# Convolution products placed around the head copies, and one reciprocal moved behind a maximum, in the attention phase of an encoder layer

## The reference, cut to what matters

```python
a = u[..., :C_CONV] * jax.nn.sigmoid(u[..., C_CONV:])
a = conv(a, conv_w, width 31, depthwise) + conv_b          # 1024 tokens x 512 channels
...
s = einsum('bqhd,bkhd->bhqk', q, k) * scale                # 8 heads, 96 wide, 1024 x 1024
p = softmax(s);  o = einsum('bhqk,bkhd->bqhd', p, v)       # v is 64 wide
```

## Time and profile before

| | |
|---|---|
| runs of the kernel | 1921.9 us median of 3 (1918.92 to 1922.35) |
| the profiled execution | 1919.46 us, its span 1917.3 us |
| PE busy | 1840.7 us (96%) |
| DVE busy | 1389.1 us (72%) |
| ACT busy | 796.2 us (42%) |
| POOL busy | 802.1 us (42%) |
| mean granted TensorE clock | 0.986 of full |

### The profile page before, as it was taken

The page is one execution under the profiler, slowest core; times in us unless marked ns, Lnnn a source line. Parts: engine busy times, 40 slices in busy tenths (PEclk is TensorE's granted clock), DMA queues, the critical chain, the costliest instruction groups (busy, mean ns, idle before and its releaser), DMA issues.

```text
span 1917.3 us, 22679 instructions
## 1 busy us (share of the span) xinstructions
PE 1840.7 (96%) x8043; PEld 1471.1 (77%) x8043; DVE 1389.1 (72%) x1774; ACT 796.2 (42%) x1248; POOL 802.1 (42%) x605
## 2 busy tenths in 40 slices
PE   4999999999999999997999998999999999999997
PEld 3788888888888878985665656877888888888886
DVE  6778888885777686776888886358656555577778
ACT  4532232223344554246776643154332323334443
POOL 1076655665200010029999941014566556520000
PEclk8999999999999999997999999999999999999999
DMA  9046666545753442000000023112233323476333
GB/s 351 19 138 199 209 220 198 192 160 206 255 194 97 131 160 71 1 1 0 1 1 0 3 73 144 66 55 91 102 110 110 110 83 110 170 251 226 99 106 126
DMA packets 132795, 232.11 MB, mean 121 GB/s; under 512 B 8780, under 2 KB 66227, under 8 KB 132434
## 3 DMA queue, kind: packets, MB, share of 16 engines
q1 hardware_dynamic: 132500, 230.73, 35.5%
q10 hardware_dynamic: 190, 0.01, 0.0%
HBM read 177.75 MB, written 52.95 MB: 120 GB/s over the span
## 4 chain that ended last, share of the span: by engine, by line
PE 35%; POOL 7%; issue 6%; DVE 5%; DMA 1%; ACT 1%; POOLq 0%; ACTq 0%; DVEq 0%
PE ps L502 19%; PE ps L854 9%; PE ps L2753 4%; POOL cv L1816 3%; PE ps L376 1%; POOL cv L1815 1%; PE ps L1657 1%; POOL slot L1766 1%; PE ps L1635 1%; DVE T L935 1%; POOL rqk L1751 0%; DMA wor<-in_w_out 0%; DVE wo L1926 0%; DVE grow L1673 0%; DVE ring L479 0%
## 5 line engine op out<-in xcount | busy, mean ns | idle before, releaser
L502 PE MATMUL ps<-T,ring 128*128 128x512 f32 x1920 | 441.8, 389 | 0.0
L502 PEld LDWEIGHTS ps<-T,ring 128*128 128x128 f32 x1920 | 360.3, 188 | 75.1 <-DVE ring L479 0.2
L502 PE MATMUL ps<-B,ring 128*128 128x512 f32 x1440 | 339.6, 392 | 4.1 <-DVE SG L561 3.8
L502 PEld LDWEIGHTS ps<-B,ring 128*128 128x128 f32 x1440 | 270.5, 189 | 63.9 <-issue 8.0
L954 POOL TENSOR_SCALAR stat<-stat 128x1 f32<-128x1 f32 x32 | 10.5, 329 | 548.7 <-ACT XS L879 257.8
L568 POOL TENSOR_TENSOR HID<-HID,SG 128x512 f32<-128x512 f32 x80 | 122.1, 1527 | 262.3 <-DVE HID L553 151.5
L854 PE MATMUL ps<-PW 128*128 128x512 f32 x924 | 217.3, 389 | 0.0
L854 PE MATMUL ps<-PT 128*128 128x512 f32 x900 | 212.0, 390 | 0.0
L854 PEld LDWEIGHTS ps<-PW 128*128 128x128 f32 x924 | 173.3, 188 | 36.0
L479 DVE TENSOR_TENSOR ring<-sums,ring 128x512 fp32r<-128x512 f32 x160 | 162.4, 1024 | 52.6 <-ACT ring L473 52.6
L854 PEld LDWEIGHTS ps<-PT 128*128 128x128 f32 x900 | 168.5, 188 | 34.8
(11 more groups left out here) (337 smaller groups left out, 3313.1 us busy)
## 6 DMA issues: line engine op xcount, KB each, us to landing
adat<-ffn_hidden SPq DMA_DIRECT2D x154, 256.0 KB, 2.7
ada_raw<-in_w_ada SPq DMA_DIRECT2D x56, 512.0 KB, 4.0
rawg<-in_ffn_wg SPq DMA_DIRECT2D x22, 1024.0 KB, 5.5
rawu<-in_ffn_wu SPq DMA_DIRECT2D x22, 1024.0 KB, 5.3
ffn_hidden<-HID SPq DMA_DIRECT2D x84, 256.0 KB, 2.8
ffn_hidden<-base SPq DMA_DIRECT2D x66, 256.0 KB, 2.6
H<-in_x SPq DMA_DIRECT2D x16, 512.0 KB, 6.6
h_saved_rows<-H SPq DMA_DIRECT2D x16, 512.0 KB, 2.6
```

The lines of the kernel that those rows point to most:

```text
L502: mm = e.matmul(ps[:, product_bank(M, k)], ring[:, place % RING, wx, kc], RIGHT[k][:, xx, kc], start=(kc == 0 and i == 0), stop=(kc == HC ...
```

## The change

Products are dealt out anew, seven to an even unit and three to an odd one, where it was six and four. A second table, `AHEAD`, says how many products of a quarter stand ahead of its row copy and exponential (behind the head copy of the same quarter); the others stand behind the exponential and the PV copy as before. In odd units of turns 0 to 2 (but not the first odd unit, which has no reciprocals) DVE's third reciprocal moves from the third quarter to the fourth, behind that quarter's maximum. POOL's list follows the products: one more sum ahead of the head scaling and one fewer behind it.

```diff
-        PRODUCTS = ((2, 1, 2, 1), (0, 1, 2, 1))
+        PRODUCTS = ((2, 2, 1, 2), (0, 1, 2, 0))
+        AHEAD = ((1, 1, 0, 1), (0, 0, 0, 0))
...
+            def act_products(i, m, p, first, behind):
+                if first and m == 0 and p == 0:
+                    return
+                of_quarter = products(m, p, p + 1)
+                ahead = AHEAD[m % NH][p]
+                for n in of_quarter[ahead:] if behind else of_quarter[:ahead]:
+                    act_prod(e, i, n, first)
...
                     if m % NH == 0 and not (last and m // NH == 1):
                         act_head_unit(e, *next_head(i, m), p)
+                    if not last:
+                        act_products(i, m, p, first, False)
                     if p == 3 and not (last and m == NU - 1):
                         act_max(e, i, m + 1)
...
-                    if not last and not (first and m == 0 and p == 0):
-                        for n in products(m, p, p + 1):
-                            act_prod(e, i, n, first)
+                    if not last:
+                        act_products(i, m, p, first, True)
...
                     if not (first and m < 2):
+                        behind = m % NH == 1 and not last
                         if p == 3:
+                            if behind:
+                                dve_pv_recip(e, *at(i, m - 1), 2)
                             dve_pv_scale(e, *at(i, m - 1))
-                        elif not (last and m == 2 and p == 2):
+                        elif not (p == 2 and (behind or last and m == 2)):
                             dve_pv_recip(e, *at(i, m - 1), p)
```

## The result

The changed kernel takes 1923.57 us in the median of 22 runs (1919.78 to 1926.36), the kernel before 1919.39 us in 22 runs beside it (1914.64 to 1925.0). The ratio is 1.0023 with a 95% interval of [1.0016, 1.0030]: by the ratio some 4.4 us slower, where 2.8 us faster was forecast. (The ratios in this document are the record's estimates. They are not quotients of the medians shown and can differ from them by up to 0.12%.) The profiled execution took 1923.23 us, its span is 1921.0 us.

What follows compares the result with a forecast made beforehand. PE and POOL were taken as both nearly full. Of 9.7 us PE could win, 7 stay with POOL; 2.5 us at the head turn plus 0.3 behind gives 2.8, from 1921.9 to 1919.1 us (own range 1917.4 to 1920.8; 8 in 10: 1913.5 to 1922.5).

Steps and rivals of the forecast that it cites:

- The ceiling: Attention pairs on PE: without PE's waits a pair takes 31.34 us, so five pairs could win 9.4 us.
- The reciprocal: Odd units on DVE: last maximum comes 1.07 us sooner, ending PE's 0.79 us wait; alone worth up to 3.9 us.
- POOL's pace without idle time: POOL in the five pairs: 32.3 us of work plus 0.6 for the first tap, 32.9 us a pair.
- the sum: Attention phase: POOL's tenth sum ends at 925.0, its sixtieth at 1089.8, head turn at 1085.2; 2.8 us won in all.
- the walk of one pair: Instructions of a pair placed where engine and wait allow: products' start times, PE not held if POOL keeps up.
- the x of 4.7 us: End of the odd unit's third product on POOL after the first head turn; PE unheld up to about 4.6 us.
- The wait only moves: Rival: PE waits as long for row or exponential, POOL's pace unchanged; 0 to 1 us won, 1921.4 us, chance 0.20.
- The first taps do not meet the sums: Rival: odd units' first taps miss POOL's sums, POOL stays at 32.3 us a pair; 1916.0 us, chance 0.22.
- The slower rival: Gathered PE waits lower the granted clock, 2.4 us a fall; 1928.3 us with one in each of five pairs; chance 0.06.
- The gap of the first pair: PE's two gaps of 1.26 and 2.50 us become one of nearly 4 us; row of maxima unchanged at 903.3 to 903.4.
- the signs: After-profile: POOL hardly idle, some 3 us busier; odd first taps 2.0 us; PE's `negmax` wait gone; head turn at 1085.
- The rule weighed: DVE and POOL port lock: each tap would stop POOL 1.28 us, not the 1.0 used; five first taps cost 1.4 us more.

Runs made afterwards that it cites:

- e8: Changed kernel with the second half of each of POOL's 60 sums left out: 1908.03 us, ratio 0.9945 to the kernel before.
- e3: Changed kernel, with POOL waiting for DVE's scaling ahead of its sixth sum of every even unit but the first: 1918.30 us, ratio 0.9986.
- e10: Changed kernel, with POOL waiting on its own semaphore between the halves of the fifth and sixth sum of each pair only: 1917.27 us, ratio 0.9986.
- e4: Changed kernel, with the even units' scaling in turns 0 to 2 replaced by a one-input reduction, division left out: 1916.19 us, ratio 0.9979.
- e11: Kernel before, with the sixth product of an even unit moved ahead of the row copy and last exponential: 1923.06 us, ratio 0.9999.
- e7: Changed kernel, with the seventh product of an even unit ahead of ACT's PV copy instead of behind it: 1935.13 us, ratio 1.0083.
- e2: Kernel before, with only the third reciprocal moved behind the last maximum, products as before: 1918.89 us, ratio 0.9989.
- e1: Changed kernel with the third reciprocal back in the third quarter, leaving only the new deal of products: 1925.64 us, ratio 1.0020.
- e6: Changed kernel, with the even units' scaling one place earlier on DVE, ahead of the fourth low part: 1945.03 us, ratio 1.0123.
- e9: Changed kernel, with each odd unit's last tap moved directly in front of the next even unit's scaling: 1925.22 us, ratio 1.0024.
- e5: Changed kernel, with POOL waiting on its own semaphore between the halves of every sum: 1922.82 us, ratio 1.0008.

## Why the prediction was wrong

**The ceiling** (31.34 us a pair on PE) was right: 31.23 to 31.32 us in e8, with half the sums left out.

**The reciprocal.** Its mechanism was right, its worth alone was not: 0.9 us in place of "up to 3.9". The wait for the last maximum went in both orders, but POOL's pace gave it back in front of another head turn.

**POOL's pace without idle time**, 32.9 us with the first tap on a running sum, was right as a pace: 32.8 to 33.2 us in the last four pairs of e3 and e10, with the stretched sum of 2.26 to 2.32 us. The terms of the sum come out in e10 too. Its phase began 2.90 us later than in the kernel before; less that, POOL's tenth sum ends at 925.1 us, the sixtieth at 1089.8 and the head turn is at 1085.3, where the sum said 925.0, 1089.8 and 1085.2. Both kernels stand to before at 0.9986, 2.7 us less, where the sum said 2.8 (under 0.2%, but with intervals that end below 1). That was not the changed kernel, though: there, with 1.29 us taken off, the sixtieth sum ends at 1095.8.

**The step that failed** is the walk of one pair: "laying each instruction of the timelines where its engine and its wait let it start", with the seventh product at "18 us" behind the head turn and "one short wait in the second pair" as POOL's only idle time. The first six products of a pair came as the walk had them: it said 2, 4, 7.2, 9.7, 12.2 and 14.7 us behind the head turn (for the x of 4.7 us measured there), and in the pair from 955.83 on they started at 2.3, 4.9, 7.4, 9.8, 12.4 and 14.8. The seventh started at 20.7, and POOL had been out of products since 19.6. In e3 and e10, where the scaling gets in, it starts at 17.9 to 18.3, as the walk said. So the term at fault is DVE's scaling, which the walk let in when it was issued or at the next end of a half, and which took 3.6 to 4.5 us. I had priced the collisions of taps with sums, by 1.0 us for POOL, and weighed a rule of two engines blocking each other for one instruction, without asking what stands behind an instruction of DVE that does not get in. In the old deal the last product of an even unit, the sixth, stood behind the PV copy too (ACT's rows at 972.59 and 973.06), but no PV copy waited for a scaling, and POOL waited 1.2 us a pair. In the new deal the PV copy waits for the scaling, and POOL waits 2.35 us a pair for the seventh. That gives the pair of 34.2 us by a sum made afterwards: POOL's 32.3, less about 0.5 because the scaling no longer stretches a sum, plus 2.35 of idle time, is 34.15. The first taps fell into this idle time as before (1.28 us, with a sum of 1.78), so the 0.6 us a pair for them wasn't paid either.

**The rivals.** None was this one. "The wait only moves" held POOL at its pace of before; here the pace itself fell. "The first taps do not meet the sums" came true, for the reason that POOL was idle. The slower rival spoke of the clock, and that stayed at 1.00 in the stretch. The gap of the first pair came as forecast, 3.71 us in one piece, and cost no further fall: from 893 to 930 us the granted clock was 0.90, for 0.91 before. The row of maxima behind it did not come at the same time as before but 1.7 us later (906.33, less the 1.29, for 903.29). The chance given to all that is slower by over 0.2% was 0.06, and all of it was the clock's. Of the signs, one came out right: PE's wait for `negmax` in odd units is gone, and the row copy is waited for.

**The rule weighed.** The Trainium skill, SBUF — State Buffer, "Who interferes with whom", has the second of two engines blocked until the first is done. A scaling of 4.53 us, held over the running half and three further ones, or one of 9.97 us, is not in it; the measurement decides. (The 1.4 us that the prediction adds by this rule make 1920.5 us, not 1920.6.) What it says of one SBUF input, that it does not contend, the trace of e4 bears out (0.68 us).

**What stays open.** What decides between a hold and a quick entry. In the changed kernel the even scalings are held and the odd ones get in at the next boundary; in the kernel before and in the later pairs of e11 the even ones get in as well; e7 has both among its even scalings, and e11 a held tap in an odd unit. The moment of issue alone doesn't separate them: in the changed kernel an even scaling issued 0.03 us after the start of a second half was held (937.52), and an odd one issued 0.02 us after the start of one got in at the next boundary (955.18). Among even scalings alone, in the kernels without gaps, the rows of DVE and POOL do tell them apart, though. Those that got in were issued 0.12 to 0.25 us into a first half or 1.14 to 1.15 us into a second one (before, e2, e7, e11). Those that were held were issued at other moments, 1.0 us and more into a first half or 0.03 to 0.7 or 1.2 us into a second one (after, e1, e7, e11). e6 adds held ones from 0.64 us on in a first half. No run moved the moment and nothing else, so its part is untested. The neighbour on DVE (e6) and the kind of operation (e9) did not end the hold. Shown is that with one SBUF input there is no hold (e4), that more ready work for POOL can make it longer (e7), that a gap of 0.1 us ends it (e5, e10), and that ending it gives the forecast's pace (e3, e10).

The last 0.9 us of the loss, behind the fifth pair, were not followed by a run. In the traces PE waits there for DVE's `pp` 3.29 us, where it waited 1.77 us before, but e10, which is faster, has such a wait too (2.98 us).

## What to carry to other kernels

Where a DVE instruction with two SBUF inputs stands between a producer and POOL's next work, reckon that it may take not its own length but up to POOL's next pause, and ask who waits behind it. It need not come so: the same scaling took 0.67 to 1.80 us at other places in turns 0 to 2 and in other orders of the program. More ready work for POOL can lengthen the hold, and the hold can then starve POOL. A wait of POOL on a semaphore of its own, put between two of its instructions at that place only, leaves about 0.1 us, and in e5 and e10 no even scaling took over 1.26 us.

## What the runs showed of the hardware

- A DVE instruction with two SBUF inputs was held not through one instruction of POOL but through seven on end (8.57 us in e11) and through eight behind the running one (9.97 us in e7). POOL's own rows are not stretched meanwhile (1.26 to 1.29 us a half).
- A hold ended in most cases when POOL ran out of work, but in e7 once between two sums without a pause (4.27 us).
- The phase, behind the same instructions, began between 869.37 and 876.08 us in different traces, so single spans compare badly here; lengths inside the phase agreed with the ratios (4.5 us for 4.4).
